# Two low-rank products side by side in every tile, and a channel mean from two products, in a two-block network on one core

## What is computed

```
# RWKV mixer: decay and rate come from two low-rank products each (64 columns in the middle)
w_log = -softplus(-(w0 + tanh(xw @ w1) @ w2)) - 0.5
a     = sigmoid(a0 + (xa @ a1) @ a2)
# convolution mixer: 31 taps per channel, then a layer norm over the 1024 channels of a token
u = glu_in[..., :1024] * sigmoid(glu_in[..., 1024:])
u = conv(u, conv_w) + conv_b
mu = mean(u, axis=-1);  y = (u - mu) * rsqrt(var(u) + 1e-5) * g + b
c_out = silu(y)
```

## Time and profile before

| | |
|---|---|
| median of 3 runs | 2098.58 us (2097.71 to 2098.59) |
| span of the profiled execution, first to last instruction | 2094.7 us |
| what lies around the span, if that execution took the median | 3.9 us |
| PE busy | 2022.0 us, 97% |
| DVE / ACT / POOL busy | 1032.5 / 784.1 / 909.8 us |
| tiles 0 to 7 of the recurrence, with the gates behind them | about 900 to 1585 us |
| mean granted TensorE clock | 0.982 |

### The profile page before, as it was taken

How to read it: one execution, slowest core, us unless ns; L and a number is a source line. 1 busy time by engine, 2 the same in 40 slices (tenths; PEclk the granted TensorE clock), 3 DMA queues, 4 the chain that set the end, 5 groups by cost and what they waited for, 6 DMA issues and landing times.

```text
span 2094.7 us, 40435 instructions
## 1 busy us (share of the span) xinstructions
PE 2022.0 (97%) x16936; PEld 1598.3 (76%) x16936; DVE 1032.5 (49%) x1763; ACT 784.1 (37%) x1298; POOL 909.8 (43%) x724
## 2 busy tenths in 40 slices
PE   6999999999999999999999999999999999999997
PEld 5876667877888888877777777777787888888886
DVE  6343553243732231688778877876614366312212
ACT  4456664223432232444333333433234334322322
POOL 5334464444545454465233223323233455545442
PEclk9989999999999999999999999999999999999998
DMA  8520013422422222331111111111132322222221
GB/s 329 191 71 11 22 41 131 181 91 81 171 99 93 101 91 101 108 114 45 38 35 58 42 37 45 48 38 38 52 124 69 135 100 91 101 92 100 101 94 67
DMA packets 53059, 187.16 MB, mean 89 GB/s; under 512 B 6032, under 2 KB 7184, under 8 KB 52624
## 3 DMA queue, kind: packets, MB, share of 16 engines
q1 hardware_dynamic: 49104, 174.49, 23.5%
q10 hardware_dynamic: 3776, 10.09, 1.3%
HBM read 178.27 MB, written 6.29 MB: 88 GB/s over the span
## 4 chain that ended last, share of the span: by engine, by line
PE 89%; DVE 4%; ACT 2%; POOL 2%; issue 2%; DMA 0%; DVEq 0%; SPq 0%; ACTq 0%; POOLq 0%
PE psum L898 24%; PE psum L900 22%; PE psum L899 22%; PE psum L1360 2%; PE psum L1044 2%; PE psum L1065 1%; PE psum L1050 1%; PE psum L1352 1%; PE psum L1294 1%; POOL wlo L774 1%; PE psum L1326 1%; PE psum L1336 1%; PE psum L1304 1%; PE psum L1366 1%; PE psum L1083 1%
## 5 line engine op out<-in xcount | busy, mean ns | idle before, releaser
L774 POOL TENSOR_TENSOR wlo<-raw,whi 128x512 fp32r<-128x512 f32 x524 | 716.9, 1389 | 949.3 <-ACT whi L1485 949.3
L898 PE MATMUL psum<-ah,whi 128*128 128x512 f32 x1256 | 520.6, 415 | 3.8 <-DVE ah L1923 3.0
L899 PE MATMUL psum<-ah,whi 128*128 128x512 f32 x1256 | 495.8, 395 | 0.0
L900 PE MATMUL psum<-ah,wlo 128*128 128x512 f32 x1256 | 495.2, 394 | 0.0
L1485 ACT ACTIVATE whi<-raw 128x1024 fp32r<-128x1024 f32 x262 | 275.9, 1054 | 322.9 <-PE psum L900 318.0
L898 PEld LDWEIGHTS psum<-ah,whi 128*128 128x128 f32 x1256 | 238.9, 190 | 67.6 <-issue 11.3
L900 PEld LDWEIGHTS psum<-ah,wlo 128*128 128x128 f32 x1256 | 239.0, 190 | 52.6
L899 PEld LDWEIGHTS psum<-ah,whi 128*128 128x128 f32 x1256 | 239.5, 191 | 42.2 <-issue 0.2
L2244 DVE SCALAR_TENSOR_TENSOR x<-upad,vec,x 128x512 f32<-128x512 f32 x240 | 211.4, 881 | 5.8
L898 PE MATMUL psum<-hidden,whi 128*128 128x512 f32 x536 | 208.7, 389 | 0.0
L900 PE MATMUL psum<-hidden,wlo 128*128 128x512 f32 x536 | 208.5, 389 | 0.0
(11 more groups left out here) (378 smaller groups left out, 2874.1 us busy)
## 6 DMA issues: line engine op xcount, KB each, us to landing
raw<-in_w SPq DMA_DIRECT2D x300, 512.0 KB, 3.4
raw_first<-in_w SPq DMA_DIRECT2D x14, 512.0 KB, 9.5
raw_ck<-in_w SPq DMA_DIRECT2D x8, 512.0 KB, 7.3
x<-in_x SPq DMA_DIRECT2D x4, 512.0 KB, 6.1
x_kept<-x ACTq DMA_DIRECT2D x1, 2048.0 KB, 10.3
ao_kept<-ao ACTq DMA_DIRECT2D x8, 256.0 KB, 2.0
aof<-ao_kept ACTq DMA_DIRECT2D x1, 2048.0 KB, 10.6
x<-x_kept ACTq DMA_DIRECT2D x1, 2048.0 KB, 8.1
```

What stands on the lines that cost most here:

```text
L774: pool.tensor_tensor(lo_weight(place(s))[:, c], raw_of(SPLITS[s])[:, c], hi_weight(place(s)).bitcast(F32)[:, c], ALU.subtract).then_inc(lo ...
L898: pe.matmul(dst, wh, h_, start=first, stop=False)
L899: pe.matmul(dst, wh, l_, start=False, stop=False)
L900: return pe.matmul(dst, wl, h_, start=False, stop=last)
```

## The change

In `tile_ahead`, step `la2` moves from behind the parts of r to right behind `lw2`. On POOL, at step `opv` of tiles 2 to 7, one addition is new: it sums the finished convolution tiles 0 to `j - 1` in `conv_sum`, which is memory of `sq_sum` that nothing else uses at that time. The channel sum then takes two matmuls in place of eight: one of `conv_sum` (tiles 0 to 6), one of tile 7.

```
     return (k
-      + [("lw2", j)] + r[:2] + [("mix", j, 1), ("scan", j)] + r[2:] + [("la2", j)] + v[:2] + [("mix", j, 0), ("kk", j)]
+      + [("lw2", j), ("la2", j)] + r[:2] + [("mix", j, 1), ("scan", j)] + r[2:] + v[:2] + [("mix", j, 0), ("kk", j)]
...
+        conv_sum = sq_sum[:, 1, :]
...
+                elif kind == "opv" and j >= 2:
+                    pool.wait_ge(conv_done, j)
+                    if j > 2:
+                        pool.wait_ge(conv_added, j - 2)
+                    pool.tensor_tensor(conv_sum, x[:, 0, :] if j == 2 else conv_sum, x[:, j - 1, :], ALU.add).then_inc(conv_added, 1)
...
             begin(("convmean",))
-            for k in range(KT):
-                pe.wait_ge(conv_done, k + 1)
-                mm = pe.matmul(bank(("convmean",)), ones, x[:, k, :], start=k == 0, stop=k == KT - 1)
-            mm.then_inc(filled, 1)
+            pe.wait_ge(conv_added, KT - 2)
+            pe.matmul(bank(("convmean",)), ones, conv_sum, start=True, stop=False)
+            pe.wait_ge(conv_done, KT)
+            pe.matmul(bank(("convmean",)), ones, x[:, KT - 1, :], start=False, stop=True).then_inc(filled, 1)
```

More of the change, by code:

```diff
@@ L146, in tile_ahead @@
     k, r, v, g = (parts(what, 4) for what in (("rkv", j, 1), ("rkv", j, 0), ("rkv", j, 2), ("glu", j, 1)))
-    return (k + [("lw2", j)] + r[:2] + [("mix", j, 1), ("scan", j)] + r[2:] + [("la2", j)] + v[:2] + [("mix", j, 0), ("kk", j)]
+    return (k + [("lw2", j), ("la2", j)] + r[:2] + [("mix", j, 1), ("scan", j)] + r[2:] + v[:2] + [("mix", j, 0), ("kk", j)]
             + v[2:3] + [("lg2", j)] + v[3:] + [("kkss", j), ("kkinv", j)] + g[:1] + [("mix", j, 2)] + g[1:2] + [("kkb", j)] + g[2:3] + [("bonus", j)]
@@ L668, in build_program @@
         conv_done, cen_ready, convn_ready = sem("conv_done"), sem("cen_ready"), sem("convn_ready")
+        conv_added = sem("conv_added")
         ao_hi, ao_ready = sem("ao_hi"), sem("ao_ready")
```

## The result

The changed kernel takes **2102.49 us** (median of 11 runs, 2099.67 to 2108.39), the kernel before on the same chip 2098.58 us (11 runs). The ratio is 1.0026, with a 95% interval of 1.0018 to 1.0034: a little slower, where I forecast 2086.8 us and faster. Its profiled execution took 2102.97 us with a span of 2100.8, so 2.2 us lie around the span and not the 3.9 that I had worked out of before's median.

The account below looks back on a forecast made before the run. PE was taken to bound the kernel, busy 2022.0 of 2094.7 us. Gains of 7.3 and 5.2 less 0.7 made 11.8 us, a span of 2082.9, plus 3.9 around it: 2086.8 us, range 2084.6 to 2090.8.

Parts of the forecast that it names:

- The pair: Decay and rate products side by side on PE: 1.04 us gained a tile, 7.3 us over tiles 1 to 7.
- The channel sum: Twelve of sixteen PE records go at 0.43 us each: 5.2 us gained.
- The addition on POOL: Six additions of about 1.26 us in POOL's idle time; taken as costing nothing, bound 7.6 us.
- the weights of `pr`: POOL's second weight block for the product after the channel sum stays in time for PE, with 2.4 us of cover.
- the 0.7 that I had taken back: PE's expected wait for DVE's `iy`, 0.1 us a tile, subtracted from the gain; ends 0 and 3.0 us.
- What is late next in the chain: PE earlier by 1.05 us, DVE by 0.38: wait at `iy` 0.1 us a tile, at most 0.43.
- The parenthesis: Aside that POOL's weight work also moves ahead and may fall on more of DVE's taps; no size of its own.
- The eviction of `rate` on ACT: Now ahead of the first `ix` copies, making them 0.69 us later; cover 0.7 us, so taken as nothing.
- DVE takes more of it back: Rival: DVE's chain from `ip` to `iy` follows PE less, costing 3.0 instead of 0.7 us; 2089.1 us, chance 0.14.
- The Trainium skill's rule: Shared DVE and POOL ports: a tap meeting the new addition is held throughout, up to 7.6 us worse; rival's chance 0.03.
- The clock rival: PE's half-clock stretches, 1.3 us each: three to six more give 2090.7 to 2094.6 us, chance 0.07.
- The other side of the forecast: Slower than before, above 2102.8 us, needing more than 12 half-clock PE stretches; chance 0.01.

Follow-up runs that it names:

- c1: Changed kernel with two taps moved from ahead of `ip` to the tile's end and `rate` evicted behind the first `ix` copies on ACT; 2086.62 us.
- c2: c1 with a second POOL addition of the same size, result unused, ahead of each one; 2087.71 us.
- a3: Changed kernel with two of the six taps ahead of `ip` moved to the tile's end in tiles 1 to 7; 2086.11 us.
- b2: Changed kernel with the eviction of `rate` put behind the first `ix` copies on ACT; 2090.32 us.
- a4: Changed kernel with taps unmoved and POOL holding back the colliding weight block until DVE has done `ip`; 2098.00 us.

## Why the prediction was wrong, by its own steps

**Right.** The pair: 1.39 us against 1.38, and the place given up, together 1.04 us a tile on PE, of which the first of the seven tiles keeps only 0.1; with DVE in time (c1) the best periods are the 71.6 forecast. The channel sum: 5.15 us against 5.2. The addition on POOL: 1.27 us each, and free as far as c2 can tell; the `kr` beside it, which reads PSUM, keeps its 0.68 us. No new wait came for `ix`, and none for the weights of `pr` (0.4 us for POOL's `wlo`, before and after). Pair, sum and a DVE in time make 2086.1 or 2086.6 us in a3 and c1, beside the forecast of 2086.8; but that was said of a kernel that lacks the third, and the nearness is in part luck: the first tile's missing 0.9 us stands against the 0.7 that I had taken back and that a DVE in time doesn't cost.

**Wrong: "What is late next in the chain".** The term was 0.1 us a tile with 0.43 as its upper end; what the runs show is 2.4 (2.0 at `ip`, 0.39 at `iy`). I looked at `iy` alone and passed over the use of `ip` ahead of it. And the upper end rested on "if it doesn't come forward at all". DVE went backward by 2.0 us. The parenthesis named the cause, that POOL's work on the weights moves ahead and may fall on more taps, but gave it no price. The rows for one were there. POOL's start against DVE's sixth tap in the kernel before is a margin of nothing (1121.67 and 1121.73), ACT's copy ahead of it stands behind the rate product's eviction and behind `inv`, so it shifts by about the 1.05 us that PE gains, and a tap that meets POOL costs more than its 0.75 us: the 2.61 for two in the earlier trace rows say 1.86 for the one. The bound from that is two taps, about 2 us a tile.

**Wrong: "The eviction of `rate` on ACT", taken as nothing.** I checked the `ix` copies behind it and not the weight copy, which stands between. It put POOL's first block on the whole scan (+0.57 us), and that brought a second tap into the second block (b2).

**The rivals.** The first, "DVE takes more of it back", had the right engine, a price nearly six times too small and the wrong place. The Trainium skill's rule (page "SBUF — State Buffer", section "SBUF: two separate sides"), that of VectorE and GpSimd the one that comes later stands still while the other's instruction runs, describes the loss. I had asked it of the added instruction only. The old ones, moved against each other, are where it worked: a tap of 0.75 us takes 1.64 to 1.78 beside a half block of about 1.25. In the trace of the changed kernel every tap longer than 1 us (51 of 240) ends 0.55 us behind the end of the POOL instruction that began ahead of it, which is what the rule says but for some 0.2 us of the tap's 0.75 that aren't held. So a tap loses 0.9 to 1.0 us here, a good part of the half block and not all of it. `kr`, with one PSUM input, is not held, also as the rule has it. The clock rival was part of it. By the traces and without any stretch the changed periods are -0.1 for the first and six times 1.35, or 8.0 us more, and with the sum's 5.2 less the total is +2.8. With the three more stretches that its trace has than before's it is +6.7. The measured ratio says +3.8 to +7.1 us, so the runs probably hold some of them; how many, the medians don't tell. The other side of the forecast, which I gave 0.01 and hung on twelve stretches, came by a wait instead.

## What to carry to other kernels

Work taken off the bounding engine can move every engine that it paces, and not all by the same amount. So list what comes earlier (here a weight block on POOL that nobody had touched), and look at what it then lies beside on the waited-for engine. An engine that is busy for three quarters of a period, as DVE is here, can have no slack in the ten microseconds that count. Read the cover between its result and the use of it, for every use in the stretch. And when an eviction moves to another place on its engine, price all that stands behind it, as far as the engines that wait for that, and not only the one result that you had in mind.

## What the hardware showed that I had not expected

The size of it. A tap of 128x512 float32 takes at most 0.75 us with no POOL instruction beside it (179 taps of the changed kernel), and 1.64 to 1.78 when a half block of POOL's began just ahead of it. The scan is held in the kernel before as well. Tile 0's has nothing of POOL's beside it:

```profile
909.52 1.22 DVE L2339 TENSOR_TENSOR_SCAN cw<-rw,sw 128x512 f32<-128x512 f32 x1 [1.00 <-ACT sw L1524]
```

The others take 1.52 or 1.82 (first period, before and changed), 1.76 or 2.33 (the later ones), by how much of POOL's half is still to come when they start; so the change added a second part to a loss that was there. A `TENSOR_SCALAR` of 0.47 us takes 1.51 (a4). So DVE's time depends on how POOL's work lies beside it, a tap in jumps of 0.9 to 1.0 us, and 0.57 us earlier on ACT go with 12 us less in the kernel (b2), half-clock stretches included. And POOL pays too: its pair of halves takes 2.52 us alone, or beside DVE operations that read PSUM, and 2.96 to 3.47 beside taps and scan.
